# A two-block float32 model on one core: the input loaded ahead of the weights, and weight units, their partners and the input moved to other SBUF addresses

## What is computed

```python
for i in range(DEPTH):                       # 2
    hn = rmsnorm(h, mix_norm_g[i])
    if i % N_MIXERS == 0:
        h = h + mamba2_mixer(hn, ...)        # hn @ w_in first: 1024 x 5152
    else:
        h = h + fox_attention(hn, ...)       # hn @ w_in: 1024 x 4112
    h = h + conv_glu_ffn(rmsnorm(h, ffn_norm_g[i]), ffn_w_up[i], ..., ffn_w_down[i])
...
# second block, on meta tokens and x: w_in, attention and convolution, w_out, then
    h = h + peer_ffn(rmsnorm_2(h, g_ffn_norm[l]), peer_wq[l], peer_keys[l], peer_u[l], peer_v[l])
```

## The kernel before

| tile | before | changed |
|---|---|---|
| raw, hi, lo of slots 0 and 1 | 128 | 512 |
| raw, hi, lo of slot 2 | 800 | 512 |
| input, high part; step from chunk to chunk | 128; 1088 | 0; 1024 |
| input, low part; step | 640; 1088 | 0; 1024 |
| input with meta tokens (second block), high / low | 128 / 640; 1088 | 0 / 512; 1088 |
| hdh, hdl, oh, ol, xdh, xdl | 320 | 0 |
| wgh and wgl, slot 0 / slot 1 | 0 / 128 | 0 / 0 |

## Time and profile before

### The profile page before, as it was taken

One profiled execution on the slowest core, in us unless ns is written; L12 is line 12 of the kernel. 1 busy time (PEld: TensorE's weight loads), 2 busy tenths in 40 slices (PEclk: granted clock), 3 DMA queues, 4 the chain that ended last, 5 costly groups with the idle time before them and its releaser, 6 DMA issues. The chain is left out here.

```text
span 1839.1 us, 34906 instructions
## 1 busy us (share of the span) xinstructions
PE 1729.6 (94%) x12587; PEld 1624.0 (88%) x12587; DVE 1077.2 (59%) x2193; ACT 816.3 (44%) x1111; POOL 912.5 (50%) x268
## 2 busy tenths in 40 slices
PE   5879999999999999999988899699999999999996
PEld 5879899999998899999677899699999978888885
DVE  5776756334353563345886880944545277777775
ACT  3446534333646543344434544444444433333332
POOL 3553476887683378886103588956666600000000
PEclk9889999999998999999988999999999999999998
DMA  5442244555453145554103466545545687777774
GB/s 181 138 138 92 92 138 161 184 182 184 162 186 113 48 159 191 183 195 171 68 1 104 141 229 232 186 151 178 185 171 175 214 263 235 239 237 237 238 236 140
DMA packets 77436, 310.78 MB, mean 169 GB/s; under 512 B 8752, under 2 KB 10288, under 8 KB 60720
## 3 DMA queue, kind: packets, MB, share of 16 engines
q1 hardware_dynamic: 74288, 304.64, 49.2%
q10 hardware_dynamic: 3072, 5.09, 0.8%
HBM read 290.82 MB, written 18.87 MB: 168 GB/s over the span
## 5 line engine op out<-in xcount | busy, mean ns | idle before, releaser
L722 POOL TENSOR_TENSOR lo<-raw,hi 128x2048 fp32r<-128x2048 f32 x128 | 588.8, 4610 | 411.8 <-ACT hi L563 338.3
L342 PE MATMUL ps<-xh,hi 128*128 128x256 f32 (+1 forms) x1984 | 569.7, 287 | 38.0 <-POOL lo L722 22.3
L343 PE MATMUL ps<-xl,hi 128*128 128x256 f32 (+1 forms) x1984 | 560.8, 283 | 0.0
L344 PE MATMUL ps<-xh,lo 128*128 128x256 f32 (+1 forms) x1984 | 560.7, 283 | 0.0
L342 PEld LDWEIGHTS ps<-xh,hi 128*128 128x128 f32 x1984 | 378.8, 191 | 41.6 <-issue 31.2
L744 POOL TENSOR_TENSOR lo<-raw,hi 128x1024 fp32r<-128x1024 f32 x128 | 321.4, 2535 | 138.5 <-ACT hi L1686 138.5
L344 PEld LDWEIGHTS ps<-xh,lo 128*128 128x128 f32 x1984 | 378.5, 191 | 0.0
L343 PEld LDWEIGHTS ps<-xl,hi 128*128 128x128 f32 x1984 | 377.9, 190 | 0.2
L1686 ACT ACTIVATE hi<-raw 128x1024 fp32r<-128x1024 f32 x256 | 264.4, 1057 | 214.7 <-PE ps L344 204.8
L2343 DVE TENSOR_TENSOR lo<-raw,hi 128x1024 fp32r<-128x1024 f32 x128 | 156.2, 1222 | 86.0 <-ACT hi L1686 86.0
L342 PE MATMUL ps<-hi,wgh 128*128 128x512 f32 x512 | 201.1, 393 | 1.1 <-DVE wgl L2354 1.1
(11 more groups left out here) (449 smaller groups left out, 3192.3 us busy)
## 6 DMA issues: line engine op xcount, KB each, us to landing
raw<-in_w_u SPq DMA_DIRECT2D x128, 512.0 KB, 4.2
raw<-in_w_v SPq DMA_DIRECT2D x128, 512.0 KB, 4.3
raw<-in_w_up SPq DMA_DIRECT2D x44, 1024.0 KB, 4.8
raw<-in_w_down SPq DMA_DIRECT2D x22, 1024.0 KB, 4.8
raw<-in_w_fox SPq DMA_DIRECT2D x16, 1024.0 KB, 5.0
act_save<-act_out SPq DMA_DIRECT2D x64, 256.0 KB, 2.0
act_in<-act_save SPq DMA_DIRECT2D x64, 256.0 KB, 3.2
raw<-in_w_xbc SPq DMA_DIRECT2D x12, 1024.0 KB, 5.0
```

The costliest lines, as they stand in the source:

```text
L342: pe.matmul(o, ah, bh, start=start, stop=False)
L343: pe.matmul(o, ah, bl, start=False, stop=False)
L344: return pe.matmul(o, al, bh, start=False, stop=stop)
L722: return g.tensor_tensor(lo[slot][:], raw[slot][:], hi[slot][:].bitcast(F32), ALU.subtract)
```

## The change

Three things. First, the opening. SP issues the input's first two quarters ahead of unit 0, then `wdt`, unit 1, the rest of `cols`, `rows`, unit 2; ScalarE's queue keeps the first gains and the last two quarters. ScalarE runs one small activation before it waits for anything but three of POOL's constants. VectorE makes the low half of unit 0 (POOL starts with unit 1) and splits `wdt` ahead of the sums of squares; ScalarE squares two quarters after the copy of unit 0 and two after that of unit 1. TensorE's first unit is written out: 16 products with the high half, wait for the low half, the 8 products with it, then the second half as before.

Second, the places of the table above. Small tiles are moved ahead of or behind the weight slots, and a phase's tiles start at a multiple of 1024.

Third, the input of the first block is `xc`/`xcl`, chunks of 256 columns over the same bytes; the form with meta tokens, `xh`/`xl`, is used by the second block alone. The meta columns are split into tiles of their own (`xmh`, `xml`), and ScalarE copies them to their places once the rest of the second block's input is split and squared.

```diff
     raw, hi, lo = [], [], []
+    iota = sb("iota", [P, P])
+    stat = sb("stat", [P, 128])
+    rs = sb("rs", [P, 3, 32])
...
+    ident = sb("ident", [P, P])
     xh_at = place["at"]
     xh = sb("xh", [P, KC, T2], F32R)
+    xl_at = place["at"]
     xl = sb("xl", [P, KC, T2], F32R)
...
+    xc = sb("xc", [P, KC, SEQ], F32R, at=xh_at)
+    xcl = sb("xcl", [P, KC, SEQ], F32R, at=xl_at + KC * META * 4)
     reuse_at = place["at"]
     ones = sb("ones", [P, P])
-    tri = sb("tri", [P, P])
-    identb = sb("identb", [P, P], BF16)
-    negm = sb("negm", [P, T2], BF16)
-    cols = sb("cols", [P, NCOLS])
...
-    phase = place["at"]
+    phase = place["at"] = (place["at"] + 1023) // 1024 * 1024
...
-        run(U_BC, "w_xbc", range(12))
+        def x_quarter(q):
+            sp.dma_start(h[:, 2 * q:2 * q + 2, :], A["x_t"][:, 2 * q:2 * q + 2, :]).then_inc(x_loaded[q], 16)
+
+        x_quarter(0)
+        x_quarter(1)
+        load(0, A["w_xbc"][0], 0)
+        sp.dma_start(wdt[:], A["w_dt"]).then_inc(wdt_loaded, 16)
+        load(1, A["w_xbc"][1], 0)
+        sp.dma_start(cols[:, KC:], A["cols"][:, KC:]).then_inc(cols_loaded, 16)
+        sp.dma_start(rows[:], A["rows"][0].partition_broadcast(P)).then_inc(rows_loaded, 16)
+        load(2, A["w_xbc"][2], 0)
+        run(U_BC + RING, "w_xbc", range(RING, 12))
...
-        lows(0, U_PEER)
+        pool.wait_ge(lo_done, 1)
+        lows(1, U_PEER)
...
+        def first_unit():
+
+            wh, wl = cv3(hi[0][:]), cv3(lo[0][:])
+            pe.wait_ge(hi_done, 1)
+            for k in range(KC):
+                if k % 2 == 0:
+                    pe.wait_ge(x_ready, k // 2 + 1)
+                pe.matmul(ps[:, 0, 0:SEQ], wh[:, k, 0:P], xc[:, k, :], start=k == 0, stop=False)
+                pe.matmul(ps[:, 0, 0:SEQ], wh[:, k, 0:P], xcl[:, k, :], start=False, stop=False)
+            pe.wait_ge(lo_done, 1)
+            for k in range(KC):
+                pe.matmul(ps[:, 0, 0:SEQ], wl[:, k, 0:P], xc[:, k, :], start=False, stop=k == KC - 1)
+            for k in range(KC):
+                if k == 4:
+                    pe_squares(pe, 0, True, True)
+                m = three(pe, ps[:, 0, SEQ:2 * SEQ], wh[:, k, P:2 * P], wl[:, k, P:2 * P], xc[:, k, :], xcl[:, k, :],
+                          k == 0, k == KC - 1)
+            m.then_inc(unit_used, 1)
...
-        for q in range(4):
+        for q in (2, 3):
             act.dma_start(h[:, 2 * q:2 * q + 2, :], A["x_t"][:, 2 * q:2 * q + 2, :]).then_inc(x_loaded[q], 16)
-        act.dma_start(cols[:, KC:], A["cols"][:, KC:]).then_inc(cols_loaded, 16)
-        act.dma_start(wdt[:], A["w_dt"]).then_inc(wdt_loaded, 16)
-        act.dma_start(rows[:], A["rows"][0].partition_broadcast(P)).then_inc(rows_loaded, 16)
+        act.wait_ge(pool_c, 3)
+        s.activation(dtv[:, 8, 0, 0:1], ones[:, 0:1], ACT.Copy)
...
             s.activation(hi[u][:], raw[u][:], ACT.Copy).then_inc(hi_done, 1)
-            if u == 0:
-                for q in range(4):
+            if u < 2:
+                for q in (2 * u, 2 * u + 1):
                     act_square(act, q, 0, h[:, 2 * q:2 * q + 2, :].rearrange("p a b -> p (a b)"))
...
             square(3)
+            s.activation(xh[:, :, 0:META], xmh[:], ACT.Copy)
+            s.activation(xl[:, :, 0:META], xml[:], ACT.Copy)
...
-            dve_acc(v, 0)
+            v.wait_ge(hi_done, 1)
+            v.tensor_tensor(lo[0][:], raw[0][:], hi[0][:].bitcast(F32), ALU.subtract).then_inc(lo_done, 1)
             v.wait_ge(wdt_loaded, 16)
             ch(v.tensor_copy(wdth[:], wdt[:]))
             sig_v(v.tensor_tensor(wdtl[:], wdt[:], wdth[:].bitcast(F32), ALU.subtract), dt_split)
+            dve_acc(v, 0)
```

More of the change, by code:

```diff
@@ L172, in build @@
     acc = sb("acc", [P, 2, SEQ])
[L173 to L175 removed]
+    tri = sb("tri", [P, P])
     xn_at = place["at"]
@@ L180, in build @@
     tmp = [sb(f"tmp{i}", [P, 512]) for i in range(4)]
-    phase = place["at"]
+    identb = sb("identb", [P, P], BF16)
+    negm = sb("negm", [P, T2], BF16)
+    cols = sb("cols", [P, NCOLS])
+    rrow = sb("rrow", [P, T2])
+    rc = sb("rc", [P, 8])
+    rows = sb("rows", [P, NROWS])
+    phase = place["at"] = (place["at"] + 1023) // 1024 * 1024
     def start_phase():
@@ L248, in build @@
     dgm = sb("dgm", [P, META])
+    hm_at = place["at"]
     hm = sb("hm", [P, KC, META])
     hmt = sb("hmt", [P, KC, META])
+    xmh = sb("xmh", [P, KC, META], F32R)
+    xml = sb("xml", [P, KC, META], F32R, at=hm_at)
     hms = sb("hms", [P, META])
@@ L358, in pe_a, with pe_b @@
         m.then_inc(unit_used, 1)
-    def pe_b(pe, s, outs, width=256, ready=None, middle=None):
+    def pe_b(pe, s, outs, width=256, x=None, ready=None, middle=None):
         wh, wl = cv3(hi[s][:]), cv3(lo[s][:])
-        for i, (o, c, m_) in enumerate(outs):
+        for i, (o, c, m_, *other) in enumerate(outs):
+            xh_, xl_ = other[0] if other else x or (xc, xcl)
             if middle is not None and i == 1:
@@ L790, in ssd @@
             for u in range(12):
[L791 to L795, removed]
+                if u == 0:
+                    first_unit()
+                else:
+                    unit_wait(pe, u)
+                    if u >= 2:
+                        pe.wait_ge(xbc_conv, u - 1)
+                    pe_a(pe, u % RING, [ps[:, u % 2, 0:SEQ], ps[:, u % 2, SEQ:2 * SEQ]])
                 if u == 1:
@@ L815, in z_unit @@
                     pe.wait_ge(z_evac, n - 1)
-                pe_b(pe, (U_Z + n) % RING, [(ps[:, n % 2, t * 256:(t + 1) * 256], META + t * P, P) for t in range(NT)])
+                pe_b(pe, (U_Z + n) % RING, [(ps[:, n % 2, t * 256:(t + 1) * 256], t * P, P) for t in range(NT)])
             def rowbc(i):
@@ L968, in fox @@
                     turn(0)
-                pe_b(pe, (U_FQ + n) % RING, [(ps[:, n % 2, t * 256:(t + 1) * 256], META + t * P, P) for t in range(NT)],
+                pe_b(pe, (U_FQ + n) % RING, [(ps[:, n % 2, t * 256:(t + 1) * 256], t * P, P) for t in range(NT)],
                      ready=8 if n == 0 else None, middle=first_heads if n == 15 else None)
@@ L1666, in routing @@
                         for c in (2 * q, 2 * q + 1):
-                            ins = s.activation(xh[:, c, META:], new_h(c), ACT.Copy)
+                            ins = s.activation(xc[:, c, :], new_h(c), ACT.Copy)
                         ins.then_inc(x_hi, 1)
```

50 lines of the change are left out of this document (23 added, 27 removed).

## The result

| | before | after |
|---|---|---|
| median of 20 runs | 1841.26 us | 1843.91 us |
| ratio after / before, 95% interval | | 1.0018 (1.0011 to 1.0025) |
| profiled execution: own time | 1840.81 us | 1841.62 us |
| its span | 1839.1 us | 1839.9 us |
| TensorE busy | 1729.6 us, 94% | 1742.2 us, 95% |

One run of the changed kernel was disturbed (2027 us, at a granted clock of 0.79) and is left out of the ratio. The forecast was 1797 us; the change made the kernel 0.18% slower, a small rise, but one whose interval leaves out no change.

The account below looks back on a forecast made before the run. TensorE was taken as the bound nearly everywhere, through its start time and matmul spacing. From 1840.8 us, 9.8 for the opening and 34 for the spacing gave 1797 us, range 1781 to 1826.

Parts of the forecast that it names:

- The opening: Start of the kernel: reordered loads and splits let TensorE start at 12.3 instead of 22.3 us, gain 9.8 us.
- the race: Opening: VectorE's wdt split against POOL's first subtraction; VectorE wins in two cases of three, losing gives 1801 us.
- The spacing: TensorE's matmul starts: constant relative places of weights and partners bring them closer together, gain 34 us after deductions.
- I take these two: Spacing assumed for the new places: 114.0 ns for 256 columns and 227.5 ns for 512 columns.
- Input streaming: Matmuls with xh and xl streaming: spacing falls from 118.6 to 114.0 ns, gain 26.5 us.
- Input stationary: Matmuls with xh and xl stationary: spacing falls from 118.3 to 114.0 ns, gain 5.2 us.
- hdh: FFN matmuls with hdh and hdl, slot 2 in one of two FFNs: 2.7 ns less each, gain 1.4 us.
- The attention outputs, left out: Output projections in slot 2: would add a little gain, not counted in the sum.
- Last stage: 512-column matmuls with weights in slot 0: 5.4 ns less each, gain 4.1 us.
- The slower one: Rival on spacing: the new places may be bad, +4.6 ns on the same matmuls, 1868 us; chance 0.05.
- Only the opening counts: Rival on spacing: new addresses do not remove the slot differences, 118 ns stays, 1831 us; chance 0.12.

Follow-up runs that it names:

- d = 256: Changed kernel with every partner of the weight tiles (whatever they are multiplied with) shifted by 256 bytes, weights kept; 1842.81 us.
- 320: Changed kernel with every partner of the weight tiles shifted by 320 bytes, weights kept; 1834.22 us.
- the rates of 64: Changed kernel with every partner of the weight tiles shifted by 64 bytes, weights kept; 1832.74 us.
- 384: Changed kernel with every partner of the weight tiles shifted by 384 bytes, weights kept; 1848.96 us.
- those of 128: Changed kernel with every partner of the weight tiles shifted by 128 bytes, weights kept; 1848.87 us.
- d = 192: Changed kernel with every partner of the weight tiles shifted by 192 bytes, weights kept; 1814.36 us, ratio 0.9857 against the kernel before.
- the two later kernels at 192: Changed kernel, partners shifted 192 bytes, wgh and wgl at distance 0: 1815.27 us; the same plus three thrown-away matmuls ahead of some long stretches: 1814.06 us.

## Why the prediction was wrong

- *The opening* was right: 12.41 for 12.3 us, the squares at 18.47 for 18.4, the race won. Alone it gave 8.4 us for 9.8. That much of the lead is still there 1600 us later.
- *The spacing* failed, and in one step: "I take these two", 114.0 at distance 192 and 227.5 at 0 for 512 columns, as the price of distance 0 for 256 columns. The argument that the slots differ only by place was right, and so was that the pace would be equal in all of them. But the distance chosen is one of the two dearest, 0 and 96: 120.0. The two prices taken side by side did not agree: above the streaming time 227.5 has 14 ns, near the 13.3 that 120.0 has, while 114.0 has 7. Read as time above streaming, the rows put distance 0 at twice what 192 costs. That this reading meets the 120.0 is in part luck, since at 192 the two widths differ (20.0 ns for 512 columns).
- *The terms* with what the traces show. Input streaming: 5760 x (120.0 - 117.9), where 117.9 is the mean over the whole trace and not 118.6, is +12.1 us for -26.5. Input stationary: 1200 x (119.9 - 118.2) = +2.0 for -5.2. hdh: 528 x 3.3 in slot 2 and 528 x 6.2 in the others, +5.0 for -1.4. The attention outputs, left out: 768 x 4.6 = +3.5. Last stage: 768 x 6.2 = -4.8 for -4.1. Sum +17.8 for -37; the layout alone measured +15.0. So the sign was wrong for every term but the last stage.
- *The rivals.* The slower one named what happened ("The new places may be the bad ones") and its threshold: "from a rise of 1.2 ns per matmul, which eats the opening". Over the 8256 matmuls that the prediction counted, the rise was 15.0 us / 8256 = 1.8 ns, and the opening was eaten. Its price, +4.6 ns on each, was two and a half times too high, because it was set as the mirror of the best place. Given 0.05, with a range that ended at 1826, it should have had far more: no row showed 256 columns held at distance 0, and one deciding unknown does not leave 0.95 for one sign.
- *What the trace before could have told.* It has 256 columns at distance 0 in single rows: with the weights in slot 0 or 1, as for all the input's units in the loop of FFN 0, the input's rows k = 0 and 4 lie there. The mean times from start to start there are 117.5 to 117.9 ns at k = 0, 118.6 at 1, 119.1 at 2, 118.1 at 3, and at k = 4 to 7 the same four again (117.5, 118.6, 119.1, 118.1). That repeat after 4 x 64 bytes points to the period of 256 before any run. It would not have given the price: the rows at distance 0 are the cheapest there, at 117.5, and held throughout the distance costs 120.0. Where the distance changes from row to row, a matmul does not take what it takes where the distance is held.
- *Only the opening counts* (1831) would have been right in its number for a kernel with the opening alone, 1829.71. By its rule from the Trainium skill, "TensorE: Matmul & The Clock Gate", Part 2, loading the next weights does not take read bandwidth from the running matmul. These runs don't fit the forecast made from it, that addresses would change nothing: the same matmuls took 113.3 to 120.0 ns by address alone. That it is the weight load's read that costs the time, no run shows.

## What to carry to other kernels

Where float32r matmuls stream 256 columns and load new weights each, read start-to-start distances, subtract the streaming time, and compare what is left by the address of moving minus stationary modulo 256. Move tiles by a few dozen bytes and measure; a place that looks tidy (0) was one of the two worst here for 256 columns and the best for 512, and 192 bytes off took the changed kernel from a ratio of 1.0018 to 0.9857, 1.6% of the whole. A price is good for the width and the constant distance at which it was seen, and for no other. And test a layout and a schedule apart: a gain of 8 us and a loss of 15 looked like almost no change.

## What the runs showed that I had not expected

- The period is 256 bytes: d = 256 gave the changed kernel's rates and time (120.0, 226.7, 1842.81 us), 320 the rates of 64, and 384 those of 128.
- At 64 and 192 there are two rates, 113.3 and 117.8 ns, and a stretch of such products with nothing in between keeps its rate over 1450 matmuls. Four runs of the kernel with d = 192 spread over 13.7 us, where seven of the kernel before spread over 4.4; but the two later kernels at 192 spread over 4.1 and 4.0 only, so a wider spread is not shown for the distance.
- Three matmuls at distance 0 in a running stretch with the partner moving brought it from 117.8 to 113.3 in three of five places, and in none of eleven with the weights moving; behind a pause they did nothing reliable. That distance 0 is what did it is not shown.
